# Attention schedule: about forty named pieces of work may be held back, four change priority

## The reference

```python
h = rms_norm(x, ln_attn_pre)
mix = hybrid_mixer(h, w_in, ...)      # 3 head groups, each rms-normed
x = x + rms_norm(mix @ w_out, ln_attn_post)
h = rms_norm(x, ln_ffn_pre)
f = (silu(h @ ffn_w_gate) * (h @ ffn_w_up)) @ ffn_w_down
x = x + rms_norm(f, ln_ffn_post)
```

## Time and profile before

| | us |
|---|---|
| median of 3 runs | 1252.41 |
| lowest, highest | 1250.11, 1258.15 |
| the profiled execution | 1252.77 |
| its span, first to last instruction | 1251.0 |
| mean granted TensorE clock | 0.993 |
| busy in the span: PE, DVE, ACT, POOL | 1217.7, 866.4, 605.7, 181.4 |
| attention part, roughly | 118 to 521 |

### The profile page before, as it was taken

One profiled execution on the slowest core, in us unless ns is written; L12 is line 12 of the kernel. 1 busy time (PEld: TensorE's weight loads), 2 busy tenths in 40 slices (PEclk: granted clock), 3 DMA queues, 4 the chain that ended last, 5 costly groups with the idle time before them and its releaser, 6 DMA issues.

```text
span 1251.0 us, 18763 instructions
## 1 busy us (share of the span) xinstructions
PE 1217.7 (97%) x6592; PEld 1042.2 (83%) x6592; DVE 866.4 (69%) x1641; ACT 605.7 (48%) x1167; POOL 181.4 (15%) x153
## 2 busy tenths in 40 slices
PE   9999999999999999999989999999999999999996
PEld 7898878888988999888878888888888888788885
DVE  6323788858878665355876657667666568897888
ACT  5432677657776566344653333333333345444343
POOL 5230111111000000011001112112122021000114
PEclk9999999999999999999999999999999999999998
DMA  6303511136842100222312232333332455743443
GB/s 234 120 1 119 118 37 49 35 110 158 182 121 77 26 18 18 68 101 100 119 42 100 94 125 67 103 127 103 108 105 72 144 193 195 259 156 115 151 169 135
DMA packets 66881, 136.93 MB, mean 109 GB/s; under 512 B 8503, under 2 KB 27199, under 8 KB 66788
## 3 DMA queue, kind: packets, MB, share of 16 engines
q1 hardware_dynamic: 66788, 135.74, 34.0%
HBM read 90.33 MB, written 28.60 MB: 95 GB/s over the span
## 4 chain that ended last, share of the span: by engine, by line
PE 79%; DVE 9%; issue 5%; ACT 3%; DMA 2%; SPq 1%; DVEq 0%; POOL 0%; ACTq 0%; POOLq 0%
PE ps L2506 32%; PE ps L2536 11%; PE ps L1097 7%; PE ps L2450 6%; PE ps L941 4%; PE ps L1077 4%; PE ps L886 3%; PE ps L960 3%; PE ps L1042 2%; PE ps L1050 2%; DVE ring L1468 2%; PE ps L975 1%; DMA m_qs<-m_qn 1%; DVE ring L1460 1%; DVE QT L2325 1%
## 5 line engine op out<-in xcount | busy, mean ns | idle before, releaser
L2506 PE MATMUL ps<-f_topH,f_W 128*128 128x512 f32 x704 | 221.0, 389 | 3.8 <-DVE f_W L2292 2.1
L2506 PEld LDWEIGHTS ps<-f_topH,f_W 128*128 128x128 f32 x704 | 132.1, 188 | 32.0 <-DVE f_W L2292 4.6
L2292 DVE TENSOR_TENSOR f_W<-f_scr,f_W 128x512 fp32r<-128x512 f32 (+1 forms) x128 | 89.9, 705 | 84.9 <-ACT f_W L2057 84.8
L2506 PE MATMUL ps<-f_topL,f_W 128*128 128x512 f32 x352 | 136.9, 389 | 0.0
L1097 PE MATMUL ps<-V,m_tw 128*128 128x66 f32 (+1 forms) x1056 | 129.2, 273 | 2.3 <-DVE m_mix_n L1518 2.2
L1097 PEld LDWEIGHTS ps<-V,m_tw 128*128 128x128 f32 x1056 | 126.3, 193 | 5.3 <-DVE m_mix_n L1518 4.3
L2536 PE MATMUL ps<-f_headH,f_W 128*128 128x512 f32 x408 | 128.0, 390 | 2.2 <-issue 1.5
L2506 PE MATMUL ps<-f_headH,f_W 128*128 128x512 f32 x352 | 114.7, 390 | 0.0
L2536 PEld LDWEIGHTS ps<-f_headH,f_W 128*128 128x128 f32 x408 | 76.6, 188 | 19.6 <-issue 2.7
L2057 ACT CAST f_W<-f_scr 128x512 fp32r<-128x512 f32 (+1 forms) x128 | 77.6, 610 | 24.6 <-PE ps L2536 15.2
L2292 DVE TENSOR_TENSOR f_W<-ring,f_W 128x512 fp32r<-128x512 f32 x60 | 59.6, 1006 | 33.4 <-ACT f_W L2057 33.3
(11 more groups left out here) (279 smaller groups left out, 2660.4 us busy)
## 6 DMA issues: line engine op xcount, KB each, us to landing
act_pairs<-QT SPq DMA_DIRECT2D x77, 256.0 KB, 4.1
m_qs<-m_qn SPq DMA_DIRECT2D x128, 128.0 KB, 2.4
ring<-in_ffn_w_up SPq DMA_DIRECT2D x22, 512.0 KB, 3.7
f_stage<-act_pairs SPq DMA_DIRECT2D x40, 256.0 KB, 3.6
ring<-in_ffn_w_gate SPq DMA_DIRECT2D x19, 512.0 KB, 4.5
f_scr<-act_pairs SPq DMA_DIRECT2D x37, 256.0 KB, 3.1
ring<-in_ffn_w_down SPq DMA_DIRECT2D x11, 512.0 KB, 5.3
f_pair_up<-in_ffn_w_down SPq DMA_DIRECT2D x11, 512.0 KB, 6.6
```

The costliest lines, as they stand in the source:

```text
L2292: dve.tensor_tensor(slot_part(s, 1), source(s), slot_part(s, 0).bitcast(F32), ALU.subtract).then_inc(lo_done, 1)
L2506: ins = pe.matmul(ps[:, bank, :], whole[:, w, cols], halves[h][:, k0 + k, col:col + HALF], start=(begins and k == 0 and w == 0 and h == 0) ...
```

## The change

A table `HELD` names pieces of work with a time in ns by which each becomes ready later in the planner's clock, and `MOVED` adds to the age of four pieces. The planner's cost of a `piece` is 6 x 231 in place of 6 x 226.5. Nothing else changes; all lines from 254 on move down by 25 and those of the programs by 28, so L1468 of before is L1496 after.

```diff
+HELD = {
+    "combine": {36: 1000},
+    "cut_hi": {14: 1500, 16: 1500, 20: 500, 22: 2500},
...
+    "stick_weights": {19: 1000, 28: 2500},
+    "weigh": {12: 1000, 126: 1500},
+}
+MOVED = {
+    "combine": {19: 60},
+    "logits": {93: 220},
+    "scores": {15: 400, 212: 180},
+}
@@ plan_attention @@
-        work[key] = (engine, cost, need, age)
+        work[key] = (engine, cost, need, age + MOVED.get(key[0], {}).get(key[1], 0))
+
+    def held(key):
+        return HELD.get(key[0], {}).get(key[1], 0)
@@
-        add(("piece", s), "pe", 6 * 226.5, needs, 1e4 + s)
+        add(("piece", s), "pe", 6 * 231, needs, 1e4 + s)
@@
-            ready[k] = 0.0
+            ready[k] = held(k)
@@
-                ready[u] = max(done[x] + (0 if x[0] == u[0] else latency[ran_on[x]][to]) for x in set(work[u][2]))
+                ready[u] = max(done[x] + (0 if x[0] == u[0] else latency[ran_on[x]][to]) for x in set(work[u][2])) + held(u)
```

More of the change, by code:

```diff
@@ L251 @@
 FIRST_LOADS = FIRST_ITEMS // 2 + 2
+HELD = {
+    "combine": {36: 1000},
+    "cut_hi": {14: 1500, 16: 1500, 20: 500, 22: 2500},
+    "cut_lo": {15: 2500},
+    "half_hi": {11: 1500},
+    "half_keep": {16: 500},
+    "keep": {18: 500, 82: 500, 96: 500},
+    "logits": {78: 500, 88: 2500, 91: 500, 107: 500, 117: 1000, 179: 1000, 181: 2500},
+    "mean_squares": {21: 2500},
+    "scores": {48: 1000, 122: 1000, 134: 1000, 139: 2500, 141: 1000, 144: 1000, 170: 2500, 180: 2500, 183: 1000, 185: 1500},
+    "softmax": {157: 500},
+    "stick_combine": {2: 1000},
+    "stick_exp": {9: 2500, 18: 1500},
+    "stick_scan": {10: 500},
+    "stick_sub": {0: 500, 8: 1000, 18: 500},
+    "stick_weights": {19: 1000, 28: 2500},
[6 more added lines that the diff above has]
+}
 def plan_attention(lay):
```

## The result

| | before | after |
|---|---|---|
| median, us | 1252.35 (1250.11 to 1258.15, 4 runs) | 1238.08 (1237.16 to 1241.59, 4 runs) |
| the profiled execution, its span, us | 1252.77, 1251.0 | 1238.16, 1236.4 |
| mean granted clock | 0.993 | 0.995 |
| busy PE, DVE, ACT, POOL, us | 1217.7, 866.4, 605.7, 181.4 | 1212.0, 861.2, 607.5, 179.1 |

The ratio is 0.9889, with a 95% interval of 0.9863 to 0.9915: 14.3 us less, where 7.6 were forecast.

A forecast was written before the change was run, and what follows sets the result against it. VectorE and TensorE were taken to alternate as the bound, with order deciding. The terms 2.5 + 0 + 1.2 + 3.0 + 0.9 = 7.6 us, off 1252.77 or the median 1252.41, gave 1245.0; range 1239 to 1254.

The forecast's parts named there:

- place C: 360 to 408 us: part of VectorE's idle time and the half clock's loss go, 3.0 us, bounds 0 and 7.2.
- place A: Seventh and eighth stick-breaking blocks, 214 to 236 us: row 24's subtraction goes ahead of row 25's scan, 2.5 us gained.
- The work stays: Whole attention part: the same instructions in another order; the new cost of a piece adds no instruction.
- At nothing by itself: Attention part: on balance four PSUM copies leave VectorE, 2.7 us over 400 us, priced at nothing by itself.
- less 1.5 of other waiting that the new order keeps: Term of place A: 2.29 us of waiting plus 1.76 of slow clock, less 1.5 of waiting that stays.
- Before place A: Stretch ahead of 214 us: a longer query DMA wait against rows reaching VectorE earlier, 0 us, bounds -1.5 to +1.5.
- Place B: End of the stick-breaking blocks, 258.44 us: TensorE's 1.18 us wait for row 30's subtraction goes, 1.2 us gained.
- Place D: Last output projection product: its 0.92 us wait for a cut is covered by two products, 0.9 us gained.
- (1) Contention: Place A, Place B, place C: GpSimd's multiplications slow VectorE's scans and cuts; gain only 3.3 us, 1249.3; chance 0.22.
- (2) Slower: 137 to 178 us: without removed pieces waits lengthen and the clock falls in new places, +2.8 us, 1255.6; chance 0.11.
- (3): All visible waits and both clock drops go, 13.3 us, and 1.5 before place A: 1238.0; chance 0.07.
- (4): Whole change does nothing that matters, since most holds end before the engine is free: 1252.4; chance 0.05.

The follow-up runs named there:

- p1: The kernel before with the planner's cost of a piece at 231 for 226.5 alone, no tables: 1253.72 us, ratio 1.0018.
- p2: The changed kernel's tables with the old cost of a piece, 226.5: 1243.21 us, ratio 0.9922.
- k1: The kernel before with five copies of the turned bank in the nsa blocks moved from VectorE to ScalarE: 1251.6 us, ratio 0.9985.
- k2: The changed kernel with four copies of the turned bank in the nsa blocks moved back from ScalarE to VectorE: 1239.49 us, ratio 0.9906.
- h1: The kernel before with the changed order and copies from `piece` 103 to `turn` 99 alone, the first part of stage 3: 1251.58 us, ratio 0.9999.
- n2: The kernel before with the changed order from `piece` 103 to `turn` 111 alone (stage 3, first nsa blocks): 1246.64 us, ratio 0.9959.
- n3: The kernel before with the changed order from `turn` 111 to the end of the attention part alone (stages 4 and 5): 1249.59 us, ratio 0.9982.
- h2: The kernel before with the changed order from `turn` 99 to `turn` 111 alone, the second part of stage 3: 1248.77 us, ratio 0.9972.
- c1: The kernel before with one swap on VectorE, the third slc block's combine ahead of the fourth out_lo: 1251.66 us, ratio 0.999.
- o1: The kernel before with three weighted sums of TensorE (82 to 84) moved between the score products of 403 to 411 us: 1255.26 us, ratio 1.0021.
- a1: The kernel before with place A alone redone, six names moved: 1249.58 us, ratio 0.9979.

## Why the prediction was wrong in size

The kernel is faster, and each named place gained. The size was half of what came. The step that failed most is the cap on place C, VectorE's idle time up to 400 us; next come the stretch from 408 us on, priced at nothing, and place A, whose sum had two terms wrong.

**The work stays; the new cost adds nothing.** The first held, the second did not: p1 loses 2 us and p2 lacks 4 to 6. The step took the cost as no instruction and overlooked that it is a price by which the whole plan is made. "At nothing by itself" for the copies held in the old order (k1, 0.3 us in the stage) and failed in the new one (k2, 2.0 us).

**Place A, 2.5 us.** `piece` 70 to `piece` 74 took 10.61 us before (225.74 to 236.35) and 6.52 after (227.03 to 233.55): 4.1 us. The mechanism was right, down to the steps on VectorE. The timeline of the kernel after, against the earlier trace rows:

```profile
220.42 1.08 DVE L1503 TENSOR_TENSOR m_rows_sb<-ps,ring 128x896 f32<-128x896 f32 x1
...
224.70 1.09 DVE L1488 SCALAR_TENSOR_TENSOR ring<-ring,ps 128x896 f32<-128x896 f32 x1
...
227.88 1.09 DVE L1503 TENSOR_TENSOR m_rows_sb<-ps,ring 128x896 f32<-128x896 f32 x1
```

Row 26 starts at 224.70 (forecast: 225.0) and its subtraction ends at 228.97 (229.3). The chain's length, 4.27 us for 4.3, was read rightly; that its place on the clock fits too is luck in part, as this profile entered the attention part 2.7 us later than before's. `piece` 72 starts at 230.81 with no wait.

Two terms of the sum failed. The lower clock was priced at 1.76 us, from the length of twelve matmuls; by the ten profiles of the old order it costs 1.1 up to `piece` 74 and 0.5 up to `piece` 77. At full clock TensorE waits more for VectorE: behind these twelve matmuls the scores start 0.64 us after the last of them in h1, for a subtraction, and 0.23 us after it before. And "less 1.5 of other waiting that the new order keeps" is not there: `piece` 70 to 74 is 3.0 us shorter than in the old order at full clock (9.55 to 6.52), more than the whole wait of 2.29. That 2.29 + 1.76 = 4.05 comes near the 4.1 of this pair is chance.

**Before place A, 0 with bounds of 1.5.** `piece` 36 to 70 gained 1.5 us, at the bound, in this pair; the ten profiles of the old order took 99.16 to 100.20 us there, and the kernel after 98.70, so it is 0.5 to 1.5. The wait for the query DMA grew as foretold, 0.52 to 1.26 us at 141.23. The stretch was 0.8 us behind at `piece` 44 and level by `piece` 59 (0.35 ahead); the gain came after. Between `piece` 74 and 77 1.0 us was given back, 0.6 of it the part of the clock's price that the old order wins back there (17.13 us at full clock, 16.55 behind the lower one).

**Place B, 1.2 us.** `piece` 77 to `scores` 48: 5.53 to 4.11, 1.4 us. The first sliding-window scores began at 255.22 (forecast 254.5 to 255), in a profile that entered the attention part 2.7 us later than before's. Stage 1: 4.1 + 1.5 - 1.0 + 1.4 = 6.0 for a forecast of 3.7.

**Place C, 3.0 us.** Measured 6.9 in the traces, 5.9 in time (n2). This is the large miss, and it has two steps. "At best its idle time, 40.00 - 36.18 = 3.8, goes" looked at VectorE up to 400 us alone, and took 2.65 of it as fixed. In the window of the whole stage, 364.2 to 420.8 us, VectorE was busy for 48.65 of 56.6 us: 7.95 idle. Its two parts, before:

```profile
364.20:400.00 35.80, 33.09 (x239) 29.10 (x237) 34.63 (x139) 29.07 (x63) 2.54 (x3) 1.00 0.36 104
400.00:420.80 20.80, 19.35 (x129) 18.55 (x130) 14.02 (x61) 10.49 (x21) 0.54 (x1) 0.84 0.20 52
```

Only 1.2 us of the idle time lie ahead of 400, and 6.8 behind it, where nobody had looked. Of the 7.95 3.2 are left. "The same work within 0.2 us" was counted to 400 us only: in the stage VectorE has 48.65 - 46.4 = 2.3 us less. Not all of that is work spared: two copies of finished blocks (1.1 us) are ScalarE's now, but the `logits` of one row (1.0 us) only stand behind `turn` 111, as the points fix TensorE's work and not VectorE's. That splits the gain into 4.7 of idle time and 2.3 of work; k1 and k2 show that the second part counts only with the first. The clock, of which I hoped for 3.0 us, costs only 2.0 of the 6.9. I read its price as half of the stretch, but VectorE, 3.53 of 6.00 busy, paced it for part.

**Place D, 0.9 us; nothing priced from 408 to the end of the last weighted sum.** Stages 4 and 5 gained 2.2 and 1.6 us in the traces, 2.9 in time (n3). The idle time that the rows show is not the whole wait. TensorE's timeline before, at the products ahead of the earlier trace rows:

```profile
514.10 1.09 PE L1108 MATMUL ps<-o_w,o_mH 128*128 128x512 f32 x4
515.02 0.62 PE L1108 MATMUL ps<-o_w,o_mL 128*128 128x512 f32 x2
515.48 1.11 PE L1108 MATMUL ps<-o_w,o_mH 128*128 128x512 f32 x4
516.43 0.62 PE L1108 MATMUL ps<-o_w,o_mL 128*128 128x512 f32 x2
517.12 1.20 PE L1108 MATMUL ps<-o_w,o_mH 128*128 128x512 f32 x4
```

A product of six matmuls starts 1.38 us after the one before it, but the next after 1.64, with no idle time shown: a matmul is shown longer than it holds the engine (the four from 514.10 end at 515.19, and the next begins at 515.02), and a wait of 0.26 us hides in that. The same in stage 4, whose windows I had taken as full, before and after:

```profile
420.80:512.60 91.80, 91.29 (x716) 84.85 (x715) 52.04 (x206) 52.17 (x91) 2.17 (x4) 1.00 0.07 19
```
```profile
410.20:499.80 89.60, 89.27 (x717) 84.66 (x715) 54.27 (x214) 53.56 (x94) 2.25 (x5) 1.00 0.07 19
```

Matmuls leave 0.51 and 0.33 us idle, which says nothing of a gain of 2.2. The weight loads leave 6.95 and 4.94: 2.0 of it. The Trainium skill, page "Perfetto Trace Analysis", section "Identifying the Most-Contended Engine", says that matmul busy time is a poor measure of how near the engine is to full, as matmuls are pipelined, and names the LDWEIGHTS busy share as one that serves. These two windows agree: 92.4% and 94.5% by it, where the matmuls show 99.4% and 99.6%.

**The rivals.** (1) Contention: fell. Twelve cuts of VectorE in stage 1 take 777 ns on average now and took 910; the scans of 256 to 896 columns sum to 34.9 us in both. It moves and doesn't grow. The Trainium skill, page "GPSIMD Engine Reference", section Specifications, names instructions with two SBUF inputs among those that contend. The traces agree: the one scan of 3.12 us at 230.88 after (2.02 at 225.82) lay beside a multiplication of 1.46 at 230.66, and the subtraction of 640 columns at 191.68, which reads PSUM and lay wholly beside one, took 0.82 us, the mean of the four of its width. (2) Slower through new drops of the clock: none in the attention part after. (3) "More" came true in its time. Its part at B (1.18, measured 1.4) holds. Those at A (4.05 for 4.1, or 3.1 with what is given back by `piece` 77) and before A (1.5 for 0.5 to 1.5) come near with the clock priced too high. Its 7.2 at C is near the 6.9 with another make-up, 3.0 of clock where 2.0 was, and stages 4 and 5 gave 3.8 in the traces where it had 0.92. So that its sum met the time to 0.1 us is luck. Its condition, VectorE nowhere late, I took for unlikely because VectorE was nearly full; but how full it is was read in windows of 40 us that end ahead of its idle time. (4) fell: the queues' order was worth 14.3 us.

What stays open: which single handover in the second half of stage 3 makes the 2.1 us of h2 behind `turn` 99, as TensorE's queue can't be taken without VectorE's (each waits for the other in a mixed order); and how the 2.2 us of stage 4 spread.

## What to carry to other kernels

Where two engines hand work to and fro, look for the gain of a better order in the idle time of the one that paces, over the whole stage to the next point where both orders have done the same work, and not over the window before the visible stall. Measure between such points, start to start, since an engine that looks full can hide a wait in every operation. A swap at the place of the stall may move the wait (c1, o1), and less load gave next to nothing here until the order let it (k1, k2): search over whole plans, with each result timed.

## What was unexpected of the hardware

A stretch of half clock does not cost half of its length: 6.8 us of it cost the stage 2.0 us and not 3.4 (56.52 against 54.52 in the same order), as VectorE paced part of it; at place A 3.4 us of it cost 0.5 us by `piece` 77. Nor is it a property of the order alone, by the six profiles of the old order named at c1, nor of the wait ahead of it, by the three of ten at a1 whose clock stayed at 1.00 behind a wait of 2.3 us. And two kernels with the same code there differed by 3.2 us at the start of the attention part (128.47 against 125.30 us); the one had a granted clock of 0.66 on average in 7 to 12 and 55 to 60 us, the other 1.00. That is 1.7 us of work lost in each, 3.4 in all, and more than most single edits here are worth.
